# Second attention: query halves stacked on all 128 array rows, and a weighted sum of 128 columns

## The chip, the cores and the metric

The kernel runs on one core of a Trainium2 chip. The metric is the device time of one execution in microseconds (us); lower is better. Three executions of the kernel before took 1341.87, 1341.02 and 1337.63 us, median 1341.02. One further view comes from the hardware profiler, of one execution with a span of 1338.6 us.

## What is computed

Two transformer blocks in a row on 256 tokens of width 1024, all in float32. The second one, `hybrid_layer`, is where the change lies:

```
h = rms_norm_2(x, norm_mix);  proj = h @ w_in
q_flat, kv_flat, g_attn, u_pool, g_merge = split(proj)
a = nsa_attention(q_flat, kv_flat, g_attn, ...) @ w_branch_attn      # 8 heads of 64, 2 key/value groups
b = pool_mixer(u_pool, pool_w, pool_scale) @ w_branch_pool
x = x + (sigmoid(ga) * a + sigmoid(gb) * b) @ w_out
x = x + square(relu(rms_norm_2(x, norm_mlp) @ w_ff1)) @ w_ff2
```

`nsa_attention` has three branches for each head: 15 compressed keys (blocks of 32 tokens with stride 16), selected blocks and a window. With 256 tokens all blocks are selected and the window covers everything, so the last two are two causal attentions over 256 keys each, with keys ks and kw. Each branch has its own softmax, and the three outputs are added with gates of their own.

## The kernel before, in words

Activations lie feature-major: 128 features on the partitions, tokens along the free axis. Every large product is split for TensorE: a float32 value v becomes hi = fp32r(v) and lo = v - hi, and `unit` (L1439) adds w_hi x_hi, w_hi x_lo and w_lo x_hi, three matmuls of the fp32r type, for 8 chunks and 2 output tiles: 48 matmuls to one 1 MB unit of weights. SyncE loads the units in a fixed order, ScalarE makes w_hi in two halves (L477), VectorE makes w_lo (L829).

The second attention doesn't use that split. Its products are float32 matmuls on the plain values, and each shows as two records (passes) in the trace. Heads are h = 0 to 7, r = h // 2 the row block of the queries `q2`, g = h % 2 the key/value group, whose 64 features are either half of the partitions (`rows`).

The order on TensorE is written out by hand. Head 0's scores and gates2 unit 0 come first; then `head` (L1768) does, for each h from 1 to 7: `scores` of h (L1729), `turns` of h-1 (L1742, eight transposes of the probabilities), one unit of "gates2", `weighted` of h-1 (L1758). The units of gates2 are independent work that covers the softmax, which runs on VectorE (`maxima` L1265, `scaled` L1287) and ScalarE (`exps` L715). Scores write two PSUM banks, which are free again when the exponentials of the head before are taken (exp_done).

Ahead of head 0 VectorE applies the rotary embedding with `rope2` (L1215) to both keys (0, 1), the first two query blocks (2, 3), the compressed keys (4) and the last two query blocks (5, 6); L1220, L1221 and L1223 are its three operations. Between them it empties the two pooling units (`pool_in`, L1232) and makes the w_lo of gates2 units 0 and 1.

GpSimd copies one query block of 256 columns to `q_cur` for each pair of heads (L457) and then runs one of four pooling groups (`pool_group`, L423). Group r thus waits for the scores of head 2r - 1 (for r = 0: for the first rotated query block, among others).

Of the kernel before, what the change touches and what calls it, by code (L numbers as in the profile page):

```python
# [6 lines left out]
F32 = mybir.dt.float32  # L7
F32R = mybir.dt.float32r
# [5 lines left out]
P = 128  # L14
D = 1024
KD = D // P
S = 256
# [82 lines left out]
def program(nc, a, out):  # L100
    with ExitStack() as ctx:
        def sb(name, shape, dt=F32):
            return ctx.enter_context(nc.sbuf_tensor(name, shape, dt))
# [46 lines left out]
        kc_r = sb("kc_r", [P, 2, NC])  # L150
        vc_tok = sb("vc_tok", [P, G2, DH])
# [40 lines left out]
        q2 = x[:, 0:4, S:NB]  # L192
        r_ff = q_cur[:, 0, :]
# [110 lines left out]
        rope2_done = sem("rope2_done")  # L304
        v2_turned = sem("v2_turned")
# [95 lines left out]
        def _(pool):  # L401
# [62 lines left out]
        def _(act):  # L464
# [236 lines left out]
            gelu(1)  # L701
            for g in range(G2):
# [110 lines left out]
        def _(dve):  # L813
# [5 lines left out]
            dve.memset(tick[:], 0.0).then_inc(o1_done, 1)  # L819
            dve.memset(vc_tok[:], 0.0).then_inc(ones_ready, 1)  # L820
# [410 lines left out]

            def pool_in(i):  # L1232
# [24 lines left out]
            rope2(4, kc_r[:, 0, :], ps_a[:, 1, 0:NC], cos2[:, last:S:CS], sin2[:, last:S:CS], kc_r[:, 1, :])  # L1257
            pool_in(1)
# [141 lines left out]
        def _(pe):  # L1400
# [328 lines left out]
            def scores(h, r, g, first=False):  # L1729
                rows = slice(g * DH, (g + 1) * DH)  # L1730
                if g == 0:
                    pe.wait_ge(qcur_ready, HQ + r + 1)
                if not first:
                    pe.wait_ge(exp_done, 2 * HQ + h)
                q = [q_cur[rows, 0, qt * P:(qt + 1) * P] for qt in range(TT)]
                own = kk2[rows, :].rearrange("p (b n) -> p b n", b=2)[:, :, 0:P]
                pe.matmul(ps_a[:, 1, 0:2 * P].rearrange("p (b n) -> p b n", b=2), q[0], own, start=True, stop=True)
# [20 lines left out]
            def weighted(h, g):  # L1758

                rows = slice(g * DH, (g + 1) * DH)  # L1760
# [7 lines left out]
            def head(h, r, g, second=False):  # L1768
                scores(h, r, g)
                turns(h - 1, second)  # L1770
                unit(r, FIRST["gates2"] + g, from_x(S))
                weighted(h - 1, 1 - g)

            scores(0, 0, 0, first=True)
            unit(0, FIRST["gates2"], from_x(S))
            head(1, 0, 1, second=True)
            head(2, 1, 0)
            with pe.Fori(1, 3) as p:
                head(2 * p + 1, p, 1)
                head(2 * p + 2, p + 1, 0)  # L1780
            head(7, 3, 1)
# [12 lines left out]
            weighted(7, 1)  # L1794
# [186 lines left out]
```

## Time and profile before

| what | value |
|---|---|
| median of three executions | 1341.02 us (1337.63 to 1341.87) |
| span of the profiled execution | 1338.6 us |
| TensorE busy | 1290.6 us (96%) |
| VectorE busy | 724.0 us (54%) |
| ScalarE busy | 588.0 us (44%) |
| GpSimd busy | 62.4 us (5%) |
| mean granted clock of TensorE | 0.977 of full |
| second attention, scores of head 0 to end of the last weighted sum | 1002.69 to 1094.00 us |

Matmuls are pipelined: the duration of one in the trace is longer than the distance from its start to the next one's. Where a sum is made, the distance between starts counts, which is what the chain of waits shows. The same holds to a lesser degree for the operations of VectorE and ScalarE, which begin before the last one's shown end.

### The profile page before, as it was taken

The numbers are of one execution on the slowest core, as the hardware profiler recorded it, in microseconds if no ns is written. First come the engines' busy times: TensorE is split into PE (matmuls) and PEld (weight loads), VectorE is DVE, ScalarE is ACT, GpSimd is POOL, SyncE is SP. The second block draws the span as 40 slices with busy tenths as digits, with TensorE's granted clock in tenths as the row PEclk, the third lists the DMA queues.
The fourth block names the chain that finished last, engine by engine and source line by source line (L and its number), as shares of the span: only waits on it lengthen the run. The fifth ranks groups of instructions, "written<-read, shape, count | busy, mean of one in ns | idle before, by whom it ended". The sixth has DMA issues, their size and how long they took to land.

```text
span 1338.6 us, 23359 instructions
## 1 busy us (share of the span) xinstructions
PE 1290.6 (96%) x8912; PEld 1147.0 (86%) x8912; DVE 724.0 (54%) x1210; ACT 588.0 (44%) x884; POOL 62.4 (5%) x72
## 2 busy tenths in 40 slices
PE   5899999999999999999998999998999999999997
PEld 3677777778887699888998999997888889999997
DVE  2533333333334765776665555655657767666664
ACT  2443223421233436554434656545434565544542
POOL 1000000000001000000001000002011201000001
PEclk7899999999999999999998999998999999999998
DMA  9544444344223344432453555544432325455542
GB/s 388 222 182 151 175 185 185 150 173 186 92 75 136 137 158 141 143 122 99 157 180 134 219 189 188 188 170 144 158 127 95 98 92 185 162 189 189 188 163 88
DMA packets 30958, 214.17 MB, mean 160 GB/s; under 512 B 3376, under 2 KB 4656, under 8 KB 5936
## 3 DMA queue, kind: packets, MB, share of 16 engines
q1 hardware_dynamic: 30032, 209.73, 43.3%
q10 hardware_dynamic: 864, 3.56, 0.7%
q8 instruction: 45, 0.74, 0.2%
q14 instruction: 17, 0.14, 0.0%
HBM read 212.23 MB, written 1.05 MB: 159 GB/s over the span
## 4 chain that ended last, share of the span: by engine, by line
PE 87%; DVE 5%; ACT 4%; DMA 2%; issue 2%; DVEq 0%; ACTq 0%; SPq 0%
PE ps_u L1455 26%; PE ps_u L1456 25%; PE ps_u L1457 25%; PE ps_a L1430 2%; PE ps_a L1413 1%; PE ps_a L1402 1%; DMA scr<-in_mods 1%; ACT w_hi L477 1%; DMA raw<-in_stream 1%; DVE w_lo L829 1%; PE ps_a L1668 1%; DVE sq L885 1%; PE ps_a L1605 1%; PE ps_a L1590 1%; PE ps_a L1764 1%
## 5 line engine op out<-in xcount | busy, mean ns | idle before, releaser
L1455 PE MATMUL ps_u<-x_hi,w_hi 128*128 128x256 f32 (+1 forms) x1744 | 545.5, 313 | 14.4 <-DVE x_lo L896 10.7
L829 DVE TENSOR_TENSOR w_lo<-raw,w_hi 128x1024 fp32r<-128x1024 f32 x322 | 394.4, 1229 | 289.7 <-ACT w_hi L477 285.3
L1456 PE MATMUL ps_u<-x_lo,w_hi 128*128 128x256 f32 (+1 forms) x1744 | 537.5, 308 | 0.0
L1457 PE MATMUL ps_u<-x_hi,w_lo 128*128 128x256 f32 (+1 forms) x1744 | 536.9, 308 | 0.0
L477 ACT ACTIVATE w_hi<-raw 128x1024 fp32r<-128x1024 f32 x322 | 336.9, 1054 | 301.4 <-PE ps_u L1457 253.7
L1455 PEld LDWEIGHTS ps_u<-x_hi,w_hi 128*128 128x128 f32 x1744 | 335.6, 192 | 44.2 <-issue 24.6
L1457 PEld LDWEIGHTS ps_u<-x_hi,w_lo 128*128 128x128 f32 x1744 | 335.5, 192 | 15.6
L1456 PEld LDWEIGHTS ps_u<-x_lo,w_hi 128*128 128x128 f32 x1744 | 335.8, 193 | 15.1 <-issue 0.5
L1455 PE MATMUL ps_u<-h_hi,w_hi 128*128 128x256 f32 (+1 forms) x800 | 246.4, 308 | 0.9 <-DVE h_lo L970 0.5
L1456 PE MATMUL ps_u<-h_lo,w_hi 128*128 128x256 f32 (+1 forms) x800 | 245.2, 307 | 0.0
L1457 PE MATMUL ps_u<-h_hi,w_lo 128*128 128x256 f32 (+1 forms) x800 | 245.0, 306 | 0.0
L1455 PEld LDWEIGHTS ps_u<-h_hi,w_hi 128*128 128x128 f32 x800 | 152.8, 191 | 11.0 <-issue 2.9
L1457 PEld LDWEIGHTS ps_u<-h_hi,w_lo 128*128 128x128 f32 x800 | 152.8, 191 | 7.0
L1456 PEld LDWEIGHTS ps_u<-h_lo,w_hi 128*128 128x128 f32 x800 | 152.8, 191 | 6.7
L408 POOL TENSOR_TENSOR sq<-sq 128x512 f32<-128x512 f32 (+1 forms) x30 | 36.7, 1222 | 974.2 <-ACT sq L529 886.9
L967 DVE TENSOR_TENSOR t<-s,ps_u 128x512 f32<-128x512 f32 (+1 forms) x44 | 24.4, 554 | 92.7 <-ACT s L563 92.7
L563 ACT ACTIVATE s<-ps_u 128x512 f32<-128x512 f32 (+1 forms) x44 | 21.5, 488 | 99.6 <-PE ps_u L1457 99.4
L929 DVE SCALAR_TENSOR_TENSOR x<-ps_u,gate_half,x 128x256 f32<-128x256 f32 x72 | 30.4, 477 | 32.6 <-PE ps_u L1457 32.5
L970 DVE TENSOR_TENSOR h_lo<-t,h_hi 128x512 f32 (+1 forms) x44 | 24.6, 559 | 36.1 <-ACT h_hi L565 36.1
L565 ACT ACTIVATE h_hi<-t 128x512 f32 (+1 forms) x44 | 23.1, 525 | 37.7 <-DVE t L967 37.7
L477 ACT ACT_TABLE_LOAD x19 | 24.4, 1283 | 17.9 <-DMA raw<-in_stream 17.7
L1430 PE MATMUL ps_a<-wide_scr,sc_pad 128*32 128x256 f32 x288 | 23.7, 463 | 7.1 <-ACT sc_pad L493 6.9
(228 smaller groups left out, 803.0 us busy)
## 6 DMA issues: line engine op xcount, KB each, us to landing
raw<-in_stream SPq DMA_DIRECT2D x153, 1024.0 KB, 4.8
wide_scr<-in_mods SPq DMA_DIRECT2D x18, 1024.0 KB, 6.7
scr<-in_mods SPq DMA_DIRECT2D x18, 1024.0 KB, 6.8
raw<-in_stream SPq DMA_DIRECT2D x8, 768.0 KB, 4.1
x<-in_tokens ACTq DMA_DIRECT2D x2, 1024.0 KB, 14.8
wide_scr<-in_cmp_w SPq DMA_DIRECT2D x2, 1024.0 KB, 7.8
sq<-in_cmp_w SPq DMA_DIRECT2D x2, 1024.0 KB, 7.5
out<-x SPq DMA_DIRECT2D x4, 256.0 KB, 2.2
```

The lines of the kernel that those rows point to most:

```text
L408: pool.tensor_tensor(sq[:, 0, 0:width], sq[:, 0, 0:width], sq[:, kc, 0:width], ALU.add).then_inc(sq_sums, 1)
L477: act.activation(w_hi[:, k % 2, cols], raw[:, k % 2, cols], ACT.Copy).then_inc(h_ready, 1)
L563: act.activation(s1[:, j, 0:n], bank(k + j, 0, n), ACT.Silu).then_inc(silu_done, 1)
L565: act.activation(h_hi[:, 2 * p + j, 0:n], t1[:, j, 0:n], ACT.Copy).then_inc(hh_done, 1)
L829: dve.tensor_tensor(w_lo[:, k % 2, cols], raw[:, k % 2, cols], w_hi[:, k % 2, cols].bitcast(F32), ALU.subtract).then_inc(l_ready, 1)
L929: ins = dve.scalar_tensor_tensor(x[:, m + t, cols], bank(b, t, n)[:, cols], gate(m + t, s), x[:, m + t, cols], ALU.mult, ALU.add)
L967: dve.tensor_tensor(t1[:, j, 0:n], s1[:, j, 0:n], bank(k + j, 1, n), ALU.mult)\
L970: dve.tensor_tensor(h_lo[:, 2 * p + (first + j), 0:n], t1[:, j, 0:n], h_hi[:, 2 * p + (first + j), 0:n].bitcast(F32), ALU.subtract).then_i ...
L1430: ins = pe.matmul(ps_a[rows, b, 0:MOD_COLS], sc_pad[:, 2 * quarter + kc, :], mod_slots[slot][:, lo:lo + MOD_COLS], start=(quarter == 0 and ...
L1455: pe.matmul(dst, wh, xh, start=(kc == 0), stop=False)
L1456: pe.matmul(dst, wh, xl, start=False, stop=False)
L1457: ins = pe.matmul(dst, wl, xh, start=False, stop=(kc == span - 1))
```

## The change

- Queries and keys of the second attention are split in hi and lo. For head h a tile of 128 rows holds q_hi on the 64 rows of its group and q_lo on the other 64 (`q2_st`). The key tiles (`k2_st`, `kc_st` for the compressed keys) hold k_hi on both halves in part a = 0, and k_lo on the group's rows with zeros on the others in part a = 1. Two fp32r matmuls add q_hi k_hi + q_lo k_hi and q_hi k_lo, in place of one float32 matmul on 64 rows. The compressed keys are padded from 15 to 16 columns.
- The weighted sum uses all 128 columns of v (both groups) instead of the group's 64 columns; only the group's half of the result is read.
- ScalarE makes the hi parts: `keys_hi` (four copies of 64x512), `queries_hi` (two of 64x256 for each r), `cmp_keys_hi` (four of 64x15). VectorE makes the lo parts: `keys_lo` (two of 64x512), `queries_lo` (two of 64x256 for each r), `cmp_keys_lo` (two of 64x15), and two memsets of 64x512.
- r = 0 and 1 and the keys are done ahead of head 0; r = 2 and 3 behind head 0, ahead of head 1.
- GpSimd doesn't copy queries any more; its four pooling groups have no wait on scores left, only on their inputs, and group 0 also on the compression of keys and values (hid_done) and the gates.
- TensorE's loop over heads is written out (the last query buffer index is no longer a register).

```diff
+        kc_st = sb("kc_st", [P, 2, G2, 16], F32R)
...
+        q2_st = x_hi[:, :, S:NB]
+        k2_st = x_lo[:, :, S:NB].rearrange("p (a g b) n -> p a g b n", a=2, g=G2)
...
             for r in range(4):
-                pool.wait_ge(rope2_done, 3 + r if r < 2 else 4 + r)
-                if r:
-                    pool.wait_ge(qk_done, HQ + 2 * r)
-                else:
-                    pool.wait_ge(hid_turned, 1)
+                if r == 0:
+                    pool.wait_ge(hid_done, 2)
                     pool.wait_ge(gt_ready, 1)
-                pool.tensor_copy(q_cur[:, 0, :], q2[:, r, :]).then_inc(qcur_ready, 1)
                 pool_group(r)
...
+            def keys_hi():
+                act.wait_ge(rope2_done, 2)
+                for g in range(G2):
+                    for half in range(2):
+                        act.activation(k2_st[half * DH:(half + 1) * DH, 0, g, :, :],
+                                       kk2[g * DH:(g + 1) * DH, :].rearrange("p (b n) -> p b n", b=2), ACT.Copy).then_inc(k2_hi, 1)
...
+            def queries_hi(r):
+                act.wait_ge(rope2_done, 3 + r if r < 2 else 4 + r)
+                for g in range(G2):
+                    rows = slice(g * DH, (g + 1) * DH)
+                    act.activation(q2_st[rows, 2 * r + g, :], q2[rows, r, :], ACT.Copy).then_inc(q2_hi, 1)
...
+            keys_hi()
             splits(0, k + 7)
+            queries_hi(0)
+            queries_hi(1)
+            cmp_keys_hi()
             splits(0, k + 8)
...
             head(0, 0, 0, None, first=True)
+            for r in range(2, R2H):
+                queries_hi(r)
...
+            def keys_lo():
+                dve.wait_ge(k2_hi, 2 * G2)
+                for g in range(G2):
+                    rows = slice(g * DH, (g + 1) * DH)
+                    dve.tensor_tensor(k2_st[rows, 1, g, :, :], kk2[rows, :].rearrange("p (b n) -> p b n", b=2),
+                                      k2_st[rows, 0, g, :, :].bitcast(F32), ALU.subtract).then_inc(k2_stacked, 1)
...
+            def queries_lo(r):
+                dve.wait_ge(q2_hi, G2 * (r + 1))
+                for g in range(G2):
+                    rows, others = slice(g * DH, (g + 1) * DH), slice((1 - g) * DH, (2 - g) * DH)
+                    dve.tensor_tensor(q2_st[others, 2 * r + g, :], q2[rows, r, :], q2_st[rows, 2 * r + g, :].bitcast(F32), ALU.subtract)\
+                       .then_inc(q2_stacked, 1)
...
             rope2(4, kc_r[:, 0, :], ps_a[:, 1, 0:NC], cos2[:, last:S:CS], sin2[:, last:S:CS], kc_r[:, 1, :])
+            for g in range(G2):
+                dve.memset(k2_st[(1 - g) * DH:(2 - g) * DH, 1, g, :, :].bitcast(F32), 0.0)
+            keys_lo()
             pool_in(1)
+            queries_lo(0)
+            cmp_keys_lo()
             for r in range(2, 4):
                 rope2(3 + r, q2[:, r, :], ps_a[:, 2 + r % 2, 0:S], cos2, sin2)
+            queries_lo(1)
...
             head(0, 0, 0, None, first=True)
+            for r in range(2, R2H):
+                queries_lo(r)
...
-            def scores(h, r, g, first=False):
-                rows = slice(g * DH, (g + 1) * DH)
-                if g == 0:
-                    pe.wait_ge(qcur_ready, HQ + r + 1)
-                if not first:
+            def scores(h, g, first=False):
+
+                pe.wait_ge(q2_stacked, h + 1)
+                if first:
+                    pe.wait_ge(k2_stacked, 2 * G2)
+                else:
                     pe.wait_ge(exp_done, 2 * HQ + h)
...
+                for a in range(2):
+                    pe.matmul(lo, q[0], k2_st[:, a, g, :, 0:P], start=(a == 0), stop=(a == 1))
                 for qt in range(TT):
-                    pe.matmul(ps_a[:, 1, 2 * P + qt * 16:2 * P + qt * 16 + NC], q[qt], kc_r[rows, 1, :], start=True, stop=True)
-                pe.matmul(ps_a[:, 0, :], q[1], kk2[rows, :], start=True, stop=True).then_inc(qk_done, 1)
+                    for a in range(2):
+                        pe.matmul(ps_a[:, 1, 2 * P + qt * 16:2 * P + qt * 16 + 16], q[qt], kc_st[:, a, g, :],
+                                  start=(a == 0), stop=(a == 1))
+                for a in range(2):
+                    ins = pe.matmul(hi, q[1], k2_st[:, a, g, :, :], start=(a == 0), stop=(a == 1))
+                ins.then_inc(qk_done, 1)
...
-                    pe.matmul(ps_a[rows, 2, 0:S], v2_tok[:, b, 0, rows], probs_t[:, 2 * b, :], start=(b == 0), stop=False)
-                    pe.matmul(ps_a[rows, 2, P:S], v2_tok[:, b, 1, rows], probs_t[:, 2 * b + 1, P:S], start=False, stop=False)
-                pe.matmul(ps_a[rows, 2, 0:S], vc_tok[:, g, :], q_cur[:, 1, :], start=False, stop=True).then_inc(pv_done, 1)
+                    pe.matmul(ps_a[:, 2, 0:S], v2_tok[:, b, 0, :], probs_t[:, 2 * b, :], start=(b == 0), stop=False)
+                    pe.matmul(ps_a[:, 2, P:S], v2_tok[:, b, 1, :], probs_t[:, 2 * b + 1, P:S], start=False, stop=False)
+                pe.matmul(ps_a[:, 2, 0:S], vc_tok[:].rearrange("p g d -> p (g d)"), q_cur[:, 1, :], start=False, stop=True)\
+                  .then_inc(pv_done, 1)
```

## Rows read from the trace of the kernel before

**Rows 1.** The page, busy time of each engine over the span:

```profile
PE 1290.6 (96%) x8912; PEld 1147.0 (86%) x8912; DVE 724.0 (54%) x1210; ACT 588.0 (44%) x884; POOL 62.4 (5%) x72
```

**Rows 2.** Chain of waits, second attention: start us, us until the next, what:

```profile
1025.89 1.03 PE ps_a L1402 x8
...
1043.24 0.58 PE ps_a L1764 x2
...
1044.04 0.43 PE ps_a L1764 x2
...
1045.12 0.63 PE ps_a L1737 x2
1045.75 0.35 PE ps_a L1739 x4
1046.10 0.95 PE ps_a L1740 x2
1047.05 1.02 PE ps_a L1402 x8
...
1053.83 0.57 PE ps_a L1764 x2
...
1087.43 1.06 PE ps_a L1787 x4
```

**Rows 3.** Chain of waits, first attention: weighted sum and turns of a head:

```profile
614.11 1.73 PE ps_a L1605 x8
...
617.55 0.87 PE ps_a L1402 x8
```

**Rows 4.** Timeline of TensorE in the first feed-forward part, columns: start, us, operation:

```profile
250.05 0.39 PE L1457 MATMUL ps_u<-x_hi,w_lo 128*128 128x512 f32 x1
250.28 0.39 PE L1455 MATMUL ps_u<-x_hi,w_hi 128*128 128x512 f32 x1
```

**Rows 5.** Busy times of a stretch; the figure before the DMA share is TensorE's clock:

```profile
1014.00:1016.00 2.00, 2.00 (x11) 2.00 (x11) 2.00 (x4) 0.49 (x1) 1.92 (x2) 0.50 0.06 12
```

**Rows 6.** Timeline of VectorE around heads 0 and 1:

```profile
998.65 0.64 DVE L1220 TENSOR_TENSOR t<-x,cst 128x256 f32<-128x256 f32 x1
...
999.66 0.89 DVE L1223 TENSOR_TENSOR x<-t 128x256 f32<-128x256 f32 x1
...
1001.31 1.22 DVE L829 TENSOR_TENSOR w_lo<-raw,w_hi 128x1024 fp32r<-128x1024 f32 x1
...
1005.72 0.43 DVE L1220 TENSOR_TENSOR t<-x,cst 128x256 f32<-128x256 f32 x1
...
1006.86 0.43 DVE L1272 TENSOR_TENSOR ps_a<-ps_a,cst 128x256 f32<-128x256 f32 x1
...
1013.03 0.58 DVE L1304 TENSOR_SCALAR pc<-sc_c,inv 128x15 f32<-128x15 f32 x2
...
1022.28 0.37 DVE L1304 TENSOR_SCALAR pc<-sc_c,inv 128x15 f32<-128x15 f32 x2
```

**Rows 7.** Timeline of VectorE in head 6, without GpSimd beside it:

```profile
1068.81 0.42 DVE L1272 TENSOR_TENSOR ps_a<-ps_a,cst 128x256 f32<-128x256 f32 x1
...
1076.39 0.15 DVE L1322 COPY tick<-cst 128x1 f32<-128x1 f32 x1
```

**Rows 8.** Groups of instructions by line and shape, VectorE, first 30 us:

```profile
L818 DVE MEMSET pc<- 128x256 f32 x1 | 0.3, 272 | 0.0
```

**Rows 9.** Timeline of ScalarE ahead of head 0:

```profile
980.67 1.55 ACT L684 ACTIVATE x<-ps_u 64x256 f32<-64x256 f32 x4 [1.76 <-PE ps_u L1457]
...
999.11 1.06 ACT L477 ACTIVATE w_hi<-raw 128x1024 fp32r<-128x1024 f32 x1 [2.95 <-PE ps_u L1457]
```

**Rows 10.** Timeline of GpSimd, first copy, a pooling operation, last operation:

```profile
998.61 0.40 POOL L457 COPY q_cur<-x 128x256 f32<-128x256 f32 x1 [68.64 <-DVE x L1223]
...
1001.57 1.54 POOL L448 TENSOR_TENSOR x<-s,x 128x256 f32<-128x256 f32 x1
...
1063.37 0.74 POOL L448 TENSOR_TENSOR x<-s,x 128x256 f32<-128x256 f32 x1
```

More of the change, by code:

```diff
@@ L304, in program @@
         rope2_done = sem("rope2_done")
+        k2_hi = sem("k2_hi_done")
+        k2_stacked = sem("k2_stacked")
+        q2_hi = sem("q2_hi_done")
+        q2_stacked = sem("q2_stacked")
         v2_turned = sem("v2_turned")
@@ L701, in _, with cmp_keys_hi @@
             gelu(1)
+            def keys_hi():
[4 more added lines that the diff above has]
+                                       kk2[g * DH:(g + 1) * DH, :].rearrange("p (b n) -> p b n", b=2), ACT.Copy).then_inc(k2_hi, 1)
+            def cmp_keys_hi():
+                act.wait_ge(rope2_done, 5)
+                for g in range(G2):
+                    for half in range(2):
+                        act.activation(kc_st[half * DH:(half + 1) * DH, 0, g, 0:NC], kc_r[g * DH:(g + 1) * DH, 1, :], ACT.Copy)\
+                           .then_inc(k2_hi, 1)
+            def queries_hi(r):
[3 more added lines that the diff above has]
+                    act.activation(q2_st[rows, 2 * r + g, :], q2[rows, r, :], ACT.Copy).then_inc(q2_hi, 1)
             for g in range(G2):
@@ L819, in _ @@
             dve.memset(tick[:], 0.0).then_inc(o1_done, 1)
+            dve.memset(kc_st[:].bitcast(F32), 0.0)
             dve.memset(vc_tok[:], 0.0).then_inc(ones_ready, 1)
@@ L1230, in queries, with cmp_keys_lo @@
                 split(0, k + 5 + g, 1)
+            def keys_lo():
[4 more added lines that the diff above has]
+                                      k2_st[rows, 0, g, :, :].bitcast(F32), ALU.subtract).then_inc(k2_stacked, 1)
+            def cmp_keys_lo():
+                dve.wait_ge(k2_hi, 4 * G2)
+                for g in range(G2):
+                    rows = slice(g * DH, (g + 1) * DH)
+                    dve.tensor_tensor(kc_st[rows, 1, g, 0:NC], kc_r[rows, 1, :], kc_st[rows, 0, g, 0:NC].bitcast(F32), ALU.subtract)\
+                       .then_inc(k2_stacked, 1)
+            def queries_lo(r):
+                dve.wait_ge(q2_hi, G2 * (r + 1))
+                for g in range(G2):
+                    rows, others = slice(g * DH, (g + 1) * DH), slice((1 - g) * DH, (2 - g) * DH)
+                    dve.tensor_tensor(q2_st[others, 2 * r + g, :], q2[rows, r, :], q2_st[rows, 2 * r + g, :].bitcast(F32), ALU.subtract)\
+                       .then_inc(q2_stacked, 1)
             def pool_in(i):
@@ L1257, in _ @@
             rope2(4, kc_r[:, 0, :], ps_a[:, 1, 0:NC], cos2[:, last:S:CS], sin2[:, last:S:CS], kc_r[:, 1, :])
+            for g in range(G2):
+                dve.memset(k2_st[(1 - g) * DH:(2 - g) * DH, 1, g, :, :].bitcast(F32), 0.0)
+            keys_lo()
             pool_in(1)
+            queries_lo(0)
+            cmp_keys_lo()
             for r in range(2, 4):
                 rope2(3 + r, q2[:, r, :], ps_a[:, 2 + r % 2, 0:S], cos2, sin2)
+            queries_lo(1)
             dve.wait_ge(gt_ready, 1)
@@ L1756, in turns, with weighted @@
                 ins.then_inc(t_done, 1)
-            def weighted(h, g):
-                rows = slice(g * DH, (g + 1) * DH)
+            def weighted(h):
                 pe.wait_ge(pta_ready, HQ + h + 1)
@@ L1763, in weighted, with head @@
                 for b in range(2):
-                    pe.matmul(ps_a[rows, 2, 0:S], v2_tok[:, b, 0, rows], probs_t[:, 2 * b, :], start=(b == 0), stop=False)
-                    pe.matmul(ps_a[rows, 2, P:S], v2_tok[:, b, 1, rows], probs_t[:, 2 * b + 1, P:S], start=False, stop=False)
-                pe.matmul(ps_a[rows, 2, 0:S], vc_tok[:, g, :], q_cur[:, 1, :], start=False, stop=True).then_inc(pv_done, 1)
-            def head(h, r, g, second=False):
-                scores(h, r, g)
+                    pe.matmul(ps_a[:, 2, 0:S], v2_tok[:, b, 0, :], probs_t[:, 2 * b, :], start=(b == 0), stop=False)
+                    pe.matmul(ps_a[:, 2, P:S], v2_tok[:, b, 1, :], probs_t[:, 2 * b + 1, P:S], start=False, stop=False)
+                pe.matmul(ps_a[:, 2, 0:S], vc_tok[:].rearrange("p g d -> p (g d)"), q_cur[:, 1, :], start=False, stop=True)\
+                  .then_inc(pv_done, 1)
+            def head(h, g, second=False):
+                scores(h, g)
                 turns(h - 1, second)
-                unit(r, FIRST["gates2"] + g, from_x(S))
-                weighted(h - 1, 1 - g)
-            scores(0, 0, 0, first=True)
+                unit(0, FIRST["gates2"] + h, from_x(S))
+                weighted(h - 1)
+            scores(0, 0, first=True)
             unit(0, FIRST["gates2"], from_x(S))
[L1776 to L1781, printed above, removed]
+            for h in range(1, H2):
+                head(h, h % 2, second=(h == 1))
             def mix(i):
@@ L1793, in _ @@
             mix(3)
-            weighted(7, 1)
+            weighted(7)
             def rows_done(kc):
```

6 lines of the change are left out of this document (3 added, 3 removed).

## The prediction

> **What bounds the kernel now.** I read the page first: TensorE is busy for 96% of the span [rows 1]. So the chain of waits of the second attention was next, 1002 to 1094 us. From head 1 on it holds TensorE and nothing else. One head is the scores of head h, the turns of head h-1, one unit of gates2 (48 matmuls) and the weighted sum of head h-1. From the weighted sum at 1043.24 to that at 1053.83 it takes 10.59 us [rows 2], and all six such steps are within 0.02 us of that. The reader is to split one step: weighted sum 1.88 (1043.24 to 1045.12), scores 1.93 (0.63 + 0.35 + 0.95), turns 1.02, unit 5.75 [rows 2]. Second, the same view of the first attention, where nothing is narrower than 128 rows or columns: the same eight fp32 passes of 256 columns go at 0.216 us each, eight turns take 0.87 [rows 3]. Third, VectorE's timeline from 997 to 1007 us: there it never pauses, and it is VectorE, not TensorE, that sets when head 0's maxima begin (1006.86) though its scores were issued at 1002.69. Until the turns of head 1 the stage has thus two clocks: VectorE's start, then TensorE's period.
>
> **TensorE's part.** Old scores: fp32 in two passes on 64 rows. New: two fp32r passes of 256 columns, four of 16, two of 512. A fp32r pass of 256 columns costs 0.12 us (the unit's 5.75 over its 48 [rows 2]), of 512 columns 0.23 [rows 4], whole-array both. A 16-column fp32r pass is in no row. From below: four fp32 passes of 15 columns on 64 rows take 0.35, so 0.09 each [rows 2]; from above: a turn is 128 columns of weights and 128 moving, 0.109 [rows 3]. The weights have 128 columns, so I take 0.11: scores 2x0.12 + 4x0.11 + 2x0.23 = 1.13 (1.04 at the low end), 0.80 less than 1.93.
>
> The first pair of a narrow group costs more than its second: 0.58 against 0.43 for L1764 [rows 2], and turns behind narrow scores take 1.02 against 0.87 in the first attention [rows 2, 3]. All these shapes become whole-array, so I take 0.15 off the weighted sum (1.73) and 0.15 off the turns (0.87). That the weighted sum has 128 columns costs nothing more: passes with 128-column weights go at the same 0.216 [rows 3] as those with 64 (0.43 a pair). New period 5.75 + 0.87 + 1.73 + 1.13 = 9.48, 1.11 less than 10.59.
>
> The Trainium skill (TensorE: Matmul & The Clock Gate, LDWEIGHTS) speaks against the wider weights: loading takes the number of columns over 1.2 in ns, row count aside, so 64 more columns are 53 ns a load. If the ten loads of a weighted sum showed, that would be an estimated 0.5 us a head, and some 4 us over eight heads. The 0.216 us pitch with 128 columns says that the load lies under the running pass.
>
> **Can VectorE follow?** In a head undisturbed by GpSimd it starts the maxima at 1068.81 and ends its last op before the head's output at 1076.54 [rows 7]; then come h_lo (0.42) and a half of w_lo (1.14 net of the overlap), 9.3 us without any waiting for TensorE. That is under 9.48, but by 0.2 only; a second cover like that doesn't exist.
>
> **The start, on VectorE.** Before maxima 0 its queue gets two memsets of 64x512 (256 columns take 0.27 [rows 8], so 0.54 each, 1.1), two key remainders of 512 columns (between 0.43 for 256 and 1.22 for 1024 [rows 6], net 0.6 each: 1.2), four query remainders of 256 columns (net 0.35: 1.4), two tiny ones (0.2): 3.9 us. Half-height ops are priced at full height, since length goes by columns: 256 columns of 64 rows take ScalarE 0.39 [rows 9]. Behind head 0 come four more query remainders, 1.4, ahead of maxima 1. So the probabilities of head 1, ready at 1022.65 now [rows 6], come 5.3 later. Nothing hides this: VectorE has no pause from 997 to 1008.9.
>
> ScalarE gets four key copies (some 0.5 each) behind the unit split of 989.8, eight query copies (0.39 [rows 9]) and four tiny ones. Three of these groups stand ahead of its split of gates2 unit 1, which moves from 999.11 [rows 9] to about 1003. VectorE, delayed by its memsets and key remainders to about 1003.7, arrives then anyway, so I cost it at nothing; should ScalarE be 1 us later, it costs that 1 us. The later query copies stand in ScalarE's wait for the turns of head 0.
>
> TensorE itself now waits in front of scores 0 (q2_stacked 1, k2_stacked 4) till about 1008. Queued behind are the scores and unit 0 of gates2; they have until the turns of head 0, now at about 1019.5, so this wait costs nothing. It idles some 5 us. In the kernel before, two pauses of under 1 us (ahead of scores 1 and of turns 0) were followed by 1.2 GHz from 1014 on [rows 5]. That slow time fell on the path: from the probabilities of head 0, at 1013.61 [rows 6], to turns 1 at 1025.89 it took 12.3 where a period is 10.6. It may fall there again and puts up to 1.7 on TensorE's arrival at turns 1, 1.0 of it behind VectorE's (below). The idling comes earlier now, with a whole unit behind it to recover in, so I leave it out of the sum and keep the 0.7 in the range.
>
> **GpSimd.** It loses four copies of q (off the path), and with them the waits that spread its four pooling groups over heads 0, 2, 4 and 6. The new waits are fulfilled at once, so all pooling, 26 ops (30 with the copies) and 18 us by the sum of their durations, the last at 1063.37 now [rows 10], runs from about 996 to 1017, on top of VectorE's start. In the kernel before the first group began at 998.61 [rows 10], and VectorE's op at 998.65 took 0.64 and that at 999.66 0.89, where the like ones of 1005.72 take 0.43 [rows 6]; GpSimd's own at 1001.57 took 1.54 [rows 10]. Between 998.6 and 1001.3 VectorE lost 0.9 in four such ops, none in w_lo. On the path stand now 19 ops with two SBUF inputs. From below: no more than today, 0. From above: each pays the 0.46 of the worst row, 8.7 - 0.9 = 7.8. I take 12 of them at 0.25, 3.0 - 0.9 = 2.0 net, nearer the mean of the four than the worst. Later heads get back at most 0.3 in each of three heads, where VectorE isn't the bound.
>
> The Trainium skill (SBUF — State Buffer, Who interferes with whom) has this rule, which speaks against the change: an op of VectorE with both inputs in SBUF and an op of GpSimd that reads SBUF lock each other out for a whole instruction. The rows of 998 to 1003 us agree; by the rule ops on PSUM inputs (ropes' second product, maxima) pay nothing.
>
> **Sum.** Probabilities of head 1: 1022.65 + 5.3 + 2.0 = 1029.95, turns 1 at 1030.0 in place of 1025.89 [rows 2]. TensorE alone would be there at 1029.0: maxima 0 at 1006.86 + 3.9 + 2.0, turns 0 another 6.75 later (1013.61 less 1006.86 [rows 6]), and 9.48 on. From turns 1 to the end of weighted sum 6: 8.35 (0.87 + 5.75 + 1.73) and five periods, 47.4: 1085.75, where it is 1087.43 now [rows 2]. That is -1.7; 0.15 more on weighted sum 7, -1.8 in all. Everything behind shifts along: merge2 and the feed-forward part are TensorE at full clock. The span goes from 1338.6 to 1336.8. The profile's span is 2.4 us under the median of 1341.02; with that kept, the time is 1339.2.
>
> **Rivals.**
> A, VectorE is the bound in the heads: at 9.7 instead of 9.3 (GpSimd's leftovers, the waits for ScalarE's w_hi, 0.5 a head) five periods cost 1.1 more: 1340.3. For it: the margin of 0.2. Against: those waits end with TensorE's own weighted sum and shrink with it. Chance 0.12.
> B, the start is cheap: no loss to GpSimd. Probabilities of head 1 at 1027.95, TensorE there at 1027.0 (turns 0 at 1017.5 and 9.48). With 0.09 for each small pass, 0.1 less a head, weighted sum 6 ends at 1083.2: -4.4 with the last head's 0.15, 1336.6. For it: in w_lo it was GpSimd that waited. Chance 0.22.
> C, slower: the shared path of VectorE and GpSimd. Each of the 19 ops pays 0.46: the start is 5.8 later than in the sum, weighted sum 6 ends at 1091.6, +4.0: 1345.0. It decides from a loss of 3.8 on, where the sum is zero. For it: pooling is packed onto just these ops; against: no more than two of four rows showed it fully. Chance 0.16.
> D, the extra 0.30 of the narrow shapes stays and the small passes take 0.15 each: seven heads gain 0.46 less, 1342.4. Against it: L1764's first and second pair. The change then doesn't do what it says. Chance 0.06.
>
> **Chances and range.** The forecast has 0.44. What a measurement of this kernel can tell from no change is 0.3%, 4.0 us: under 1337.0 or over 1345.0. B is astride the lower edge, C the upper; with the scatter of the runs shown (1337.63 to 1341.87): faster 0.22, same 0.63, slower 0.15. The likeliest case alone spans 1337.5 to 1341; the range must reach B and most of C: 1335.5 to 1344.5.
>
> **What would show it.** Scores 0 on TensorE at about 1008 to 1009 (1002.69 now); maxima 0 at 1012.8; turns 1 at 1030; then a period of 9.5 us, with no extra on the first pair of a weighted sum, and scores of 1.1; GpSimd done by 1020; two-input ops of VectorE of 0.6 to 0.9 between 997 and 1012. The sum is wrong if maxima 0 starts before 1011 (B) or after 1015 (C), if TensorE shows idle time in each head (A), or if the period is above 9.8 without idle time (D).

## The result, and the profile after

The changed kernel takes 1344.64 us (median of six runs, 1342.77 to 1346.56), the kernel before, run beside it, 1340.28 (six runs, 1337.63 to 1341.87). The ratio is 1.0030, 95% interval [1.0019, 1.0042]: slower by about 4 us. Forecast was 1339.2, with a range of 1335.5 to 1344.5. So the sign is wrong, and the time lies just above the range.

The page of the kernel after, busy time and TensorE's share as in [rows 1]: TensorE does 4.6 us less work, VectorE 7.2 and ScalarE 6.4 more, and the span is longer.

```profile
span 1344.8 us, 23366 instructions
## 1 busy us (share of the span) xinstructions
PE 1286.0 (96%) x8912; PEld 1151.0 (86%) x8912; DVE 731.2 (54%) x1225; ACT 594.4 (44%) x900; POOL 62.3 (5%) x68
```

For the whole study I measure the second attention from a fixed mark, the start of VectorE's w_lo of the second query unit's first half (987.59 in the kernel before, 987.68 after). "Maxima 0" and "turns 1" are the distances from there to the first maxima of head 0 and the transposes of head 1; "a head" is a fifth of the way from turns 1 to turns 6; "last sum" is the distance to the start of head 7's weighted sum. The median is of the runs of one kernel. The kernels were timed in five groups, and the ratio is against the kernel before in the same group, whose medians lie between 1339.36 and 1340.28; so times of different groups are best compared by their ratios.

| kernel | maxima 0 | turns 1 | a head | last sum | median us | ratio, 95% interval |
|---|---|---|---|---|---|---|
| before | 19.27 | 38.23 | 10.58 | 104.47 | 1340.28 | 1 |
| after | 27.16 | 46.18 | 10.10 | 110.15 | 1344.64 | 1.0030 [1.0019, 1.0042] |
| e1_pool_spread | 24.26 | 44.47 | 10.16 | 108.74 | 1344.34 | 1.0038 [1.0026, 1.0050] |
| e2_head_lo_first | 27.16 | 45.00 | 9.71 | 106.63 | 1341.82 | 1.0020 [1.0009, 1.0031] |
| e3_no_prep | 19.03 | 37.57 | 9.88 | 100.45 | 1335.84 | 0.9972 [0.9962, 0.9983] |
| e4_wide_sum | 19.27 | 38.08 | 10.45 | 103.45 | 1338.42 | 0.9994 [0.9981, 1.0006] |
| e5_all_moved | 21.01 | 39.24 | 10.13 | 103.24 | 1337.97 | 0.9977 [0.9967, 0.9988] |
| e6_order_and_pool | 23.82 | 42.64 | 10.15 | 106.73 | 1341.59 | 1.0019 [1.0008, 1.0031] |
| e7_before_lo_first | 19.28 | 36.67 | 10.58 | 102.90 | 1339.48 | 0.9996 [0.9985, 1.0007] |
| e8_narrow_sum | 27.16 | 46.20 | 10.20 | 110.65 | 1344.66 | 1.0042 [1.0027, 1.0057] |
| e9_start_short | 17.39 | 36.58 | 10.12 | 100.54 | 1335.90 | 0.9969 [0.9959, 0.9979] |
| e10_start_short_packed | 18.93 | 38.60 | 9.64 | 99.87 | 1335.23 | 0.9960 [0.9946, 0.9975] |
| e11_before_start_short | 17.20 | 35.49 | 10.57 | 101.70 | 1337.81 | 0.9984 [0.9973, 0.9995] |
| e12_scores_early | 26.62 | 46.02 | 9.80 | 108.49 | 1343.78 | 1.0031 [1.0018, 1.0044] |
| e13_bank3_first | 18.93 | 38.52 | 9.52 | 98.85 | 1334.63 | 0.9965 [0.9953, 0.9977] |
| e14_lo_first_bank3_first | 27.16 | 44.57 | 9.53 | 104.97 | 1340.01 | 1.0005 [0.9995, 1.0014] |

The stage itself is 5.7 us longer after the change: turns 1 come 8.0 later, and the heads behind them give only 2.3 back.

The chain of waits after the change in an undisturbed head, beside [rows 2] (columns: start, us to the next, what; 1829 to 1831 are the weighted sum, 1799 to 1805 the scores, 1461 the turns):

```profile
1063.24 0.43 PE ps_a L1831 x2
1063.67 0.24 PE ps_a L1799 x2
1063.91 0.34 PE ps_a L1802 x4
1064.25 0.56 PE ps_a L1805 x2
1064.92 1.06 PE ps_a L1461 x8
1071.74 0.43 PE ps_a L1829 x2
```

The scores are 0.24 + 0.34 + 0.56 = 1.14 us, where they were 1.93; the first pair of the weighted sum costs 0.43 like every other. This is the gain on TensorE, and it is as forecast. Next to it stand two things that are not: 0.11 us of nothing ahead of the turns (1064.81 to 1064.92), and turns that still take 1.06.

The same view at head 1, the costliest place:

```profile
1031.92 0.28 DVE pc L1361 x2
1032.20 0.20 DVE w_lo L859
...
1033.25 0.14 DVE tick L1379
1033.39 0.33 DVE h_lo L1367
1033.72 0.14 issue
1033.86 1.21 PE ps_a L1461 x8
1035.07 0.21 PE ps_u L1514
```

The probabilities of head 1 are there at 1032.2, but the turns start at 1033.86. They wait for h_lo of head 0, whose reading frees the PSUM bank that the turns write (o2_done), and that operation stands in VectorE's queue behind a half of w_lo and the tick. TensorE had stood 2.4 us by then. The matmuls behind go at 0.21 instead of 0.12 us: 1.2 GHz. Busy times of that stretch in the form of [rows 5], with a granted clock of 0.58:

```profile
1034.00:1038.00 4.00, 4.00 (x23) 4.00 (x23) 3.38 (x9) 1.81 (x8) 0.00 (x0) 0.58 0.47 147
```

VectorE's timeline ahead of head 0, the rows that answer to [rows 6] (columns: start, duration, operation):

```profile
1002.97 1.66 DVE L1266 TENSOR_TENSOR x_lo<-scr,x_lo 64x512 fp32r<-64x512 f32 x2
1004.66 1.23 DVE L859 TENSOR_TENSOR w_lo<-raw,w_hi 128x1024 fp32r<-128x1024 f32 x1
...
1007.88 1.37 DVE L1280 TENSOR_TENSOR x_hi<-x,x_hi 64x256 fp32r<-64x256 f32 x2
1009.28 0.69 DVE L1273 TENSOR_TENSOR kc_st<-kc_r,kc_st 64x15 fp32r<-64x15 f32 x2
1010.00 0.75 DVE L1250 TENSOR_TENSOR t<-x,cst 128x256 f32<-128x256 f32 x1
...
1014.84 0.43 DVE L1329 TENSOR_TENSOR ps_a<-ps_a,cst 128x256 f32<-128x256 f32 x1
```

The maxima start 7.9 us later than in the kernel before, behind a list of new operations, some of them stretched (0.75 where [rows 6] has 0.43).

### The profile page after: what moved, and what is told of

Read it like the earlier page. It is cut to its first block, busy times and chain, and to the rows that moved or that the text cites. A ratio compares the mean times of both kernels' runs of the same rounds, so it can differ in the third digit from the quotient of the medians.

```text
span 1344.8 us, 23366 instructions
## 1 busy us (share of the span) xinstructions
PE 1286.0 (96%) x8912; PEld 1151.0 (86%) x8912; DVE 731.2 (54%) x1225; ACT 594.4 (44%) x900; POOL 62.3 (5%) x68
## 4 chain that ended last, share of the span: by engine, by line
PE 79%; DVE 8%; ACT 6%; DMA 4%; issue 3%; DVEq 0%; ACTq 0%; SPq 0%
PE ps_u L1514 24%; PE ps_u L1515 23%; PE ps_u L1516 23%; DMA raw<-in_stream 3%; PE ps_a L1489 2%; ACT w_hi L480 2%; DVE w_lo L859 2%; PE ps_a L1472 1%; DMA scr<-in_mods 1%; PE ps_a L1461 1%; PE ps_a L1727 1%; DVE sq L915 1%; ACT L566 1%; PE ps_a L1664 1%; PE ps_a L1478 1%
```

## The experiments

**GpSimd spread out again (e1).** The loss could be VectorE and GpSimd meeting.

```diff
             for r in range(4):
+                pool.wait_ge(rope2_done, 3 + r if r < 2 else 4 + r)
                 if r == 0:
...
+                else:
+                    pool.wait_ge(qk_done, HQ + 2 * r)
                 pool_group(r)
```

> The changed kernel with GpSimd's pooling groups held back as in the kernel before (group 0 until the first rotated query block, groups 1 to 3 until the scores of heads 1, 3 and 5); only the waits differ, no query copies come back. Theory: part of the lost time is VectorE and GpSimd meeting ahead of head 0, where VectorE's two-input operations took 0.6 to 0.9 us each instead of 0.42 to 0.45. Groups 1 to 3 leave that stretch, so the first maxima come some 2.5 us earlier than in the changed kernel (1012.3 instead of 1014.8) and the run is 2 to 2.5 us under the changed kernel (about 1342.3). Rival 1, the meeting is all of the loss: 5 us or more under it (1339). Rival 2, it is VectorE's own longer list: no difference (1344.6).

Maxima 0 come 2.9 us earlier, as the theory has it, but of that 1.7 is left at turns 1 and 1.4 at the last sum, and the runs show nothing (1344.34 against 1344.64). Group 1 now meets the four query remainders behind head 0: they take 2.49 us in e1 where they took 1.77. The meeting is real, but moving it to the heads doesn't pay. Rival 1 falls, and the theory's 2 us at the end with it; on the time it is rival 2's figure that came, though not for its reason.

**The place of h_lo (e2), and what it is in the kernel before (e7).**

```diff
                 scaled(h, r, g)
+                if not first:
+                    head_lo(h - 1, *before)
                 split(r, kg + 2, 0)
                 dve.wait_ge(g2_copied, h + 1)
                 dve.tensor_copy(tick[:], eps).then_inc(drained, 1)
-                if not first:
-                    head_lo(h - 1, *before)
                 split(r, kg + 2, 1)
```

> The changed kernel, with VectorE's h_lo of the head before placed directly behind the probabilities instead of behind the first half of w_lo and the tick. Theory: turns of head 1 waited 2.4 us for that h_lo, 1.5 us longer than for the probabilities, and TensorE then ran a unit's first third at 1.2 GHz. With the order changed turns 1 start 1.3 to 1.5 us earlier, and if the slow clock goes too, 2.5 to 3 us are gained: about 1342. Rival: the chain of VectorE (maxima of head 2 behind both halves of w_lo) arrives when it did and takes the place of that wait by head 2: under 0.5 us, 1344.3.

> The kernel before, with h_lo directly behind the probabilities. There TensorE arrives at the turns 0.1 us after that h_lo or later in every head, so the theory (the place of h_lo costs only where VectorE is the late one) says within 1 us of the kernel before. Rival: the place of h_lo held up the heads of the kernel before, too: 2 us faster or more.

In the changed kernel the move is worth 2.8 us of the median (1341.82) and 3.5 of the stage: turns 1 come 1.2 earlier, TensorE stands there 1.2 us instead of 2.4 and keeps its full clock behind (granted 1.00 over 1032 to 1038). The gain in the stage is what carries this; by the ratios, 1.0020 against 1.0030 in another group, the run gains less, and the two intervals overlap. In the kernel before it is worth nothing that the runs tell (0.9996). So this wait belongs to the changed kernel. The stage of e7's profile is 1.6 us shorter than that of before, all between turns 0 and turns 1, where TensorE kept its clock this time; on that see the last section.

**TensorE's part alone (e3).** This is e1 with everything left out that makes hi and lo; the matmuls stay, on old contents of the tiles.

```diff
-            keys_hi()
...
-            queries_hi(0)
-            queries_hi(1)
-            cmp_keys_hi()
...
-            for g in range(G2):
-                dve.memset(k2_st[(1 - g) * DH:(2 - g) * DH, 1, g, :, :].bitcast(F32), 0.0)
-            keys_lo()
...
-                pe.wait_ge(q2_stacked, h + 1)
```

> As e1_pool_spread, but the preparation is left out: no copies of keys and queries to the hi parts on ScalarE, no memsets and no lo parts on VectorE, and no waits of TensorE for them. The scores are therefore taken from old contents of the tiles, with all matmuls in place. It shows what TensorE's part is worth alone. Theory: the heads run at 9.8 us instead of 10.6, six of them 4.6 us, and the start is that of the kernel before: 5 us under the kernel before, 1335.4. Rival 1, VectorE binds the heads as soon as TensorE is quicker: periods of 10.2 or more and 1338. Rival 2, the forecast's 9.48 holds when nothing comes late: 1333.4.

1335.84 against 1344.34 for e1, the same kernel with the preparation: it costs 8.5 us where it stands, and what TensorE gains by the new matmuls, against the kernel before, is 4.0 us of the stage (0.9972, 3.8 us of the run). The theory's 5 is somewhat too much, because heads with GpSimd beside them take up to 10.2.

**The two halves of the gain (e4, e8).** e4 is the kernel before with the 128-column sum alone, e8 the changed kernel without it.

```diff
-                    pe.matmul(ps_a[rows, 2, 0:S], v2_tok[:, b, 0, rows], probs_t[:, 2 * b, :], start=(b == 0), stop=False)
+                    pe.matmul(ps_a[:, 2, 0:S], v2_tok[:, b, 0, :], probs_t[:, 2 * b, :], start=(b == 0), stop=False)
...
```

> The kernel before with one part of the change alone: the weighted sum on all 128 columns of v. Theory: the first pair of a weighted sum costs 0.43 instead of 0.58 us, because the array no longer changes its shape there; the scores still change it on their side. 0.15 us in each of eight heads: 1.2 us under the kernel before, 1339.1. Rival 1: the change of shape is only moved, the first pair of the scores takes the 0.15 as well: 1340.3. Rival 2: wider weights show in each pass: 0.5 us a head more, 1344.

> The changed kernel with the weighted sum back on 64 columns, all else kept. Theory: the array changes its shape twice more in a head (into the sum and out of it), 0.15 us each; in heads where VectorE is the late one nothing shows, in the four or so others 0.3: 1 us over the changed kernel, 1345.6. Rival 1, the forecast's: 0.3 in all heads, 2.4 us. Rival 2: the 128 columns are worth nothing, same time.

The heads of e4 take 10.45 instead of 10.58, 1.0 us of the stage; the runs are too coarse for it (0.9994, the interval has 1 in it). e8 is 0.5 longer than after in the stage, and its runs (1344.66) don't tell it from after. In its trace the first pair of the sum is back at 0.58, and the first pair of the scores behind it takes 0.43 instead of 0.24: the narrow sum costs 0.15 going in and 0.19 coming out. Little of that reaches the period of a head (10.20 against 10.10), because the longer scores cover a wait ahead of the turns that the last experiments are about (in e8 the turns of one head, at 1074.56, take 0.87). The wide sum alone is thus worth 0.13 us a head in the kernel before (e4), and 0.5 us in all in the changed kernel.

**The meeting taken away wholly (e6).** e2, and pooling groups only behind the exponentials of heads 0, 2, 4 and 6.

```diff
+                pool.wait_ge(exp_done, 2 * HQ + 2 * r + 1)
                 pool_group(r)
```

> The changed kernel with h_lo directly behind the probabilities (as e2) and the pooling groups behind the exponentials of heads 0, 2, 4 and 6, so that GpSimd is idle through all of VectorE's list ahead of head 0. Theory: the meeting costs 3 us ahead of head 0 (maxima 0 at +5 instead of +8 against the kernel before), of which 1 to 1.5 comes back as the groups now meet VectorE later: 1.5 to 2 us under e2. Rival 1, the meeting costs nothing once VectorE's chain is long: same as e2. Rival 2, all 3 us arrive at the end.

Rival 1 is right about the end: 1341.59 against 1341.82 of e2, stage 106.73 against 106.63, though the start is 3.3 us shorter (maxima 0 at 23.82 instead of 27.16). VectorE in e6, same operations as above:

```profile
999.93 1.34 DVE L1267 TENSOR_TENSOR x_lo<-scr,x_lo 64x512 fp32r<-64x512 f32 x2
...
1004.52 0.87 DVE L1281 TENSOR_TENSOR x_hi<-x,x_hi 64x256 fp32r<-64x256 f32 x2
1005.42 0.37 DVE L1274 TENSOR_TENSOR kc_st<-kc_r,kc_st 64x15 fp32r<-64x15 f32 x2
1005.82 0.42 DVE L1251 TENSOR_TENSOR t<-x,cst 128x256 f32<-128x256 f32 x1
```

0.87 instead of 1.37, 0.37 instead of 0.69, 0.42 instead of 0.75: this is what the meeting costs an operation. The heads then pay: five of them take 50.7 us instead of 48.5. The Trainium skill (SBUF — State Buffer, Who interferes with whom) says that a VectorE operation with two SBUF inputs contends with a GpSimd operation that reads SBUF, and that one with at most one SBUF input doesn't. These rows agree, and so does the ropes' product with a PSUM input (L1251 in the changed kernel), which keeps its 0.41 with GpSimd beside it.

**TensorE's wait in front of scores 0 (e12).** The prediction costed it at nothing.

```diff
             keys_lo()
-            pool_in(1)
             queries_lo(0)
             cmp_keys_lo()
+            pool_in(1)
```

> The changed kernel with the lo parts of queries 0 and 1 and of the compressed keys ahead of the emptying of the second pooling unit: TensorE's wait in front of scores 0 shrinks from 7.3 us to 3 to 4, the length of VectorE's list stays. Theory: that wait is hidden, because turns 0 wait for VectorE's probabilities: within 0.7 us of the changed kernel, 1344.6. Rival: it is TensorE's standing and its lower clock afterwards that cost: 2 us or more under the changed kernel.

The wait shrinks from 7.3 to 3.3 us, and turns 1 come at 46.02 instead of 46.18. That is "hidden", as forecast. The last sum is 1.7 earlier all the same. TensorE now stands 3.8 us in front of scores 1 and has a granted clock of 0.50 from 1018 to 1022, still ahead of turns 1; in front of turns 1 it stands 1.0 us at most and keeps its full clock behind them (granted 1.00 from 1032 to 1038). The runs (1.0031 against 1.0030) don't show it. Inconclusive beyond the first sentence.

**The preparation moved (e5), the start cut (e9, e10), the same cut in the kernel before (e11).** e5 moves memsets and keys into earlier pauses, queries 2 to 7 into the wait for the exponentials.

```diff
             def queries(g):
                 split(0, k + 5 + g, 0)
+                if g == 1:
+                    keys_lo()
...
-            queries_lo(1)
...
                 if not first:
                     turned_probs(h - 1)
+                if first:
+                    queries_lo(1)
+                    queries_lo(2)
+                elif h == 1:
+                    queries_lo(3)
                 scaled(h, r, g)
...
```

> The whole change is kept, with its preparation moved off VectorE's list ahead of head 0: memsets into VectorE's pause of some 9 us around 975, hi and lo of the keys into the pauses at 987 and 989, lo of the queries of heads 2 to 7 into the pauses in which VectorE waits for the exponentials of heads 0 and 1, w_hi of gates2 unit 1 ahead of ScalarE's last query copies, pooling groups behind the exponentials of heads 0, 2, 4 and 6, h_lo directly behind the probabilities. Theory: the change lost by where its preparation stands. Then maxima 0 come 1.3 us later than in the kernel before instead of 8, the heads run at 9.6 to 9.8 us, and the stage ends some 5 us earlier than in the kernel before: 1335, some 9 us under the changed kernel. Rival: the preparation costs what it costs wherever it stands, since VectorE is the engine next in line in every head; then no better than 1339.

1337.97, ratio 0.9977, 6.7 us under the changed kernel: the same arithmetic in another order is faster than the kernel before. That is well short of the 1335 expected, but better than the rival's 1339: the stage ends 1.2 us earlier than before, not 5. The heads take 10.13 where 9.6 to 9.8 was expected, and maxima 0 come 1.7 later than before (expected 1.3), turns 0 by 3.5. TensorE had stood 3.3 us in front of scores 0, ran the unit behind them at 1.2 GHz (granted 0.50 from 1006 to 1012) and needed 8.75 us from the last scores of head 0 (1007.18) to the scores of head 1 (1015.93). It showed no wait in front of turns 0, so there the wait in front of scores 0 does cost. e9 takes that up; its main edits against the changed kernel are:

```diff
             rope2(4, kc_r[:, 0, :], ps_a[:, 1, 0:NC], cos2[:, last:S:CS], sin2[:, last:S:CS], kc_r[:, 1, :])
-            for g in range(G2):
-                dve.memset(k2_st[(1 - g) * DH:(2 - g) * DH, 1, g, :, :].bitcast(F32), 0.0)
-            keys_lo()
-            pool_in(1)
             queries_lo(0)
             cmp_keys_lo()
-            for r in range(2, 4):
-                rope2(3 + r, q2[:, r, :], ps_a[:, 2 + r % 2, 0:S], cos2, sin2)
-            queries_lo(1)
+            pool_in(1)
...
+                if first:
+                    for q in range(2, 4):
+                        rope2(3 + q, q2[:, q, :], ps_a[:, 2 + q % 2, 0:S], cos2, sin2)
+                elif isinstance(h, int) and h in (1, 2, 3):
+                    queries_lo(h)
                 scaled(h, r, g)
...
```

> As e5_all_moved, with VectorE's list ahead of head 0 cut further: only the lo parts of queries 0 and 1 and of the compressed keys stand there, ahead of the emptying of the second pooling unit; the rotary steps of the last two query blocks stand in the pause in which VectorE waits for head 0's exponentials, the lo parts of queries 2 to 7 in those of heads 1 to 3. Theory: in e5_all_moved TensorE stood 3.3 us in front of scores 0 and fell to 1.2 GHz for unit 0 of gates2, which made it the late one at turns 0. Here it should not stand there at all, keep its full clock, and turns 0 should come within 0.5 us of the kernel before (26.1 us behind the w_lo at 987.6), the heads at 9.7 us: stage 5 us shorter than before, 1335, 3 us under e5_all_moved. Rival 1: the pooling groups in the heads hold VectorE up (10.4 us periods in e5_all_moved) and take the gain: 1337. Rival 2: VectorE's pauses in the heads aren't free, since each is followed by the operation that TensorE waits for: as e5_all_moved or slower.

> As e9_start_short, with the pooling groups free to run as soon as their input is there, as in the changed kernel. Theory: what of VectorE's list is left ahead of head 0 has few two-input operations, so they lose 1 to 1.5 us there and save 0.5 to 1 us in each of the four heads that GpSimd no longer disturbs: 1 to 2 us under e9_start_short. Rival: the meeting ahead of head 0 costs 3 us as it did in the changed kernel and the heads give nothing back: 2 us over e9_start_short.

> The kernel before with the same two moves that don't belong to the change: the rotary steps of the last two query blocks behind the maxima of head 0, and h_lo directly behind the probabilities. It tells what of e9_start_short is due to the change. Theory: maxima 0 and turns 0 come 2 us earlier, the heads stay at 10.58 us, since TensorE bounds them: 2 us under the kernel before, 1338.3. Rival: the start isn't on the path in the kernel before either, no difference.

e9 has no stand in front of scores 0 and comes to 1335.90, 2.1 under e5 (by the ratios 1.1, with intervals that overlap; in the stage 2.7). Turns 0 come at 25.48, 0.6 earlier than before, but the heads take 10.12 and not 9.7: its rival 1 has that part. e10, with GpSimd packed at the start, is 1335.23; the difference to e9 is within the scatter, but the traces show both sides of it: maxima 0 1.5 later, heads at 9.64 instead of 10.12. e11 gains 0.16% of itself by the two moves; its heads stay at 10.57. Maxima 0 come 2.1 earlier as expected, turns 0 only 1.2 (24.90 from the mark, 26.07 before); another 1.6 of its stage lies between turns 0 and turns 1, where TensorE, with no pause ahead of scores 1 and turns 0, kept its full clock (granted 1.00). So, by the ratios, of e10's 5.4 us (0.9960 of 1340) some 2 are the reordering and some 3 the change. Where TensorE bounds, the change is worth most of what it promised: 0.94 us a head in e10, of 1.11.

**What stands ahead of the turns (e13, e14).** Also in e10 a head takes 9.57 to 9.67, not 9.48, with the gap ahead of the turns. The timeline of e2 between two heads:

```profile
1059.19 0.60 PE L1831 MATMUL ps_a<-q_cur,vc_tok 128*128 128x256 f32 x2
...
1059.91 0.38 ACT L762 ACTIVATE h_hi<-ps_a 64x256 f32 x1 [1.01 <-PE ps_a L1831]
...
1060.46 0.43 DVE L1367 TENSOR_TENSOR h_lo<-ps_a,h_hi 64x256 f32 x1 [0.47 <-ACT h_hi L762]
...
1061.03 0.85 PE L1461 MATMUL ps_a<-cst,scr 128*128 128x128 f32 x6
```

The weighted sum ends at 1059.79, h_hi, h_lo, turns follow each other, 1.24 us in all; the scores in between take 1.14. That is a head which ScalarE and VectorE run in a loop, with a period of 9.80; in the last ones, which are written out, the same chain takes 1.01 (1069.59 to 1070.60) and the period is 9.57. The test puts the four transposes that go to the other bank first.

```diff
-                else:
+                for b in range(2):
+                    turn(ps_a[:, 3, b * P:(b + 1) * P], probs_lo[:, b, :])
+                for qt in range(TT):
+                    turn(ps_a[:, 3, (2 + qt) * P:(3 + qt) * P], pc[:, qt, :])
+                if not first:
+                    pe.wait_ge(o2_done, h)
                 for b in range(2):
                     for kt in range(2):
                         c = 2 * b + kt
-                        turn(ps_a[:, 2, c * P:(c + 1) * P], probs_hi[:, b, kt * P:(kt + 1) * P])
-                for b in range(2):
-                    turn(ps_a[:, 3, b * P:(b + 1) * P], probs_lo[:, b, :])
-                for qt in range(TT):
-                    ins = turn(ps_a[:, 3, (2 + qt) * P:(3 + qt) * P], pc[:, qt, :])
+                        ins = turn(ps_a[:, 2, c * P:(c + 1) * P], probs_hi[:, b, kt * P:(kt + 1) * P])
```

> As e10_start_short_packed, with the four transposes that write the PSUM bank not used by the weighted sum first, and the wait for h_lo only ahead of the other four. Theory: the heads are bounded by the chain weighted sum, h_hi, h_lo, turns, which the shorter scores no longer cover; 0.4 us of transposes now cover it, so the periods go from 9.67 (loop heads) and 9.57 to 9.5 or a little less, 1 us in all: 1334.2. Rival: the 0.2 us ahead of the turns are TensorE's own; the periods stay at 9.57 to 9.67.

> As e2_head_lo_first (the changed kernel, h_lo directly behind the probabilities), with the same order of the transposes. Theory: turns 1 no longer wait for h_lo at all, and the periods go from 9.8 and 9.57 to 9.5: 0.5 + 1.2 us under e2_head_lo_first, 1340. Rival: no change, since VectorE's probabilities come last in each head: 1341.8.

From turns 1 to turns 6 every period of e13 is 9.52, and the gap is gone. Its chain of waits:

```profile
1063.54 0.43 PE ps_a L1833 x2
1063.97 0.23 PE ps_a L1801 x2
1064.21 0.34 PE ps_a L1804 x4
1064.55 0.57 PE ps_a L1807 x2
1065.12 0.87 PE ps_a L1463 x8
```

The turns take 0.87, as in the first attention [rows 3]. e13 has the lowest median of the study, 1334.63, ratio 0.9965; the two that differ by this order alone, e13 and e10, aren't apart in the runs (0.9965 and 0.9960), only in the traces (1.0 us). e14 is the changed kernel with nothing but two orders changed, one on VectorE and one on TensorE: 1340.01, 1.0005 of the kernel before [0.9995, 1.0014], 4.6 us under the changed kernel, and 1.7 us of the stage under e2.

## Why the prediction was wrong, step by step

At the start of the last weighted sum the forecast was 1.7 us earlier than before, and the profile has 5.7 later. The 7.4 us between them are four terms.

**TensorE's part** held. Scores 1.13 forecast, 1.14 measured; weighted sum 1.73 and 1.75 (1071.74 to the next scores at 1073.49); the small pass of 16 columns, taken at 0.11 between bounds of 0.09 and 0.11, is 0.085 (0.34 for four), just under the lower one. Turns of 0.87 and a head of 9.5 are what TensorE needs, and e13 shows both, 0.87 and 9.52. e3 shows that this part is worth 4 us.

**The start, VectorE's list**, was undersized, and is 2.2 us of the difference. The probabilities of head 1 were to come 7.3 us later and came 9.5 later (44.52 from the mark instead of 35.06). Three of its terms are off. Ahead of the maxima 3.9 was forecast; e6, where nothing meets, has maxima 0 at 23.82, the kernel before without the 0.9 of its own meeting at 18.4, so 5.4. I had taken the net distance of overlapping operations (0.35 for a query remainder), while new ones follow each other at 0.44 (1.77 for four behind head 0, forecast 1.4), and the key copies of ScalarE pushed w_lo of the first gates2 unit back by 1.1 us, to 994.67, of which 0.4 arrived at VectorE's ropes. Those copies were listed at "some 0.5" each, and the four take 2.58. The meeting with GpSimd: forecast 2.0 net, measured 27.16 - 23.82 - 0.9 = 2.4. This term was about right.

**A wait that I didn't put in**, 1.6 us. The sum let turns 1 start with the probabilities. The turns wait for o2_done as well, and h_lo of the head before begins 1.1 us behind the probabilities in VectorE's queue and ends 1.5 behind them. In the kernel before no pause of TensorE's matmuls in this stage is put down to it, so no row of the waits told of it; only the code line did (`pe.wait_ge(o2_done, h)`). Whenever VectorE becomes the late engine, every wait on it has to be looked at at its place in the queue, not only the one that was the last before. e2 against after shows it: with h_lo directly behind the probabilities the stage is 3.5 us shorter, 1.2 by the wait itself and the rest by what follows from it and from the same place in later heads.

**The clock behind turns 1**, 1.5 us: 11.30 from turns 1 to turns 2, where e2, which keeps its clock, takes 9.80. I had left slow time out of the sum, with the argument that TensorE's idling comes early, ahead of head 0. It did (7.3 us, then a granted clock of 0.50 from 1008 to 1014), and was covered there; but the longer stand in front of turns 1 (2.4 us) had a slow stretch of its own.

**The heads**, the remaining 2.1 us. 9.48 was forecast, 9.6 to 9.95 measured. 0.8 of it goes with the place of h_lo again: ahead of turns 3 and turns 7 TensorE waits for an h_lo that stands behind a half of w_lo (0.7 us in both), and e2 goes from turns 2 to the last sum in 51.8 us where the changed kernel takes 52.7. The other 1.3 come because the shorter scores no longer cover the chain weighted sum, h_hi, h_lo, turns. VectorE's work as such is not too long for a head, as rival A had it: in e13 and e14, with the same work, it follows at 9.52. "Turns behind narrow scores take 1.02 against 0.87" was read as a price of the array's shape alone. That reading wasn't wrong: in e7, where h_lo comes earlier, the turns still take 1.02, and in e13, without the wait, 0.87. But in the changed kernel a new wait of 0.1 to 0.3 us took its place.

Of the rivals, C named the right side and nearly the right time (1345.0) for the wrong reason. The meeting of VectorE and GpSimd costs 3.3 us at the start, and taking it away changes the end by 0.1 (e6 against e2), since the pooling costs the heads the same. B falls with maxima 0, which come later than the forecast and not earlier. No rival had the pair of facts that decided: the preparation costs 8.5 us where it stands (e3 against e1), and it stands in front of the stretch in which VectorE sets the time; moved into pauses it costs little, though e13's 0.9965 with it against e3's 0.9972 without it has the gain of the other moves in it too. D falls with e4 and with the scores of 1.14. Of the wait in front of scores 0, "costs nothing" is right for the changed kernel (e12) and wrong for e5, where VectorE's list was short.

Not settled: how the 8.5 us divide between ScalarE's copies and VectorE's operations, which no run parted.

## What to carry to other kernels

A saving on the busiest engine is worth only what its neighbours let through, at both ends: the operations that prepare the cheaper form must not stand where another engine sets the time, and every wait that the shortened step used to cover must be priced again. List what the next engine has queued ahead of each semaphore that the busy engine waits for; the wait that ends last after a change is often one that never showed before. When a change loses this way, its order is worth trying before it is dropped: two orders changed brought e14 back to the kernel before, and the preparation moved into pauses made e13 0.35% faster than it. Of that, 0.16% comes in the kernel before too, by two of the same moves (e11).

## What the runs showed of the hardware

TensorE's clock behind the same short pauses wasn't the same in two profiles. In the profile of the kernel before, TensorE stood 0.4 us for the exponentials and 0.6 us for the probabilities of head 0, and then had a granted clock of 0.50 over 1014 to 1016 [rows 5]. In e7 the same two waits were as long:

```profile
PE ps_a L1402 <- DVE pc L1304: 0.6, 1, 0.6
PE ps_a L1737 <- ACT sc_c L724: 0.4, 1, 0.4
```

(columns: who waited for whom, us in total, times, longest), and the clock stayed at 1.00 throughout; turns 0 to turns 1 took 10.58 instead of 12.16. The instructions of these two kernels are the same up to there; what e7 changes comes a head later. In e4, again with the same two waits, turns 0 to turns 1 took 12.02, with a granted clock of 0.59 over 1014 to 1016. So a difference of 1.6 us between two single profiles of this stage can be the clock's alone, which is as much as several of the differences above, and the row of the kernel before in the table has it in it. Why it fell in one and not in the other, no run here shows.
